# Two-layer encoder trunk on one core: sums of squares of the differential heads and the memory key heads taken from split squares as two float32r products

## The reference, cut to what matters

```python
def rms_norm(x, g):
    xf = x.astype(jnp.float32)
    y = xf * lax.rsqrt(jnp.mean(xf * xf, axis=-1, keepdims=True) + EPS)
    return (y * g.astype(jnp.float32)).astype(x.dtype)

def cross_attention(h, m, w_q, w_kv, w_o, q_norm, k_norm):
    ...
    kv = (m @ w_kv).astype(f32).reshape(bsz, m.shape[1], 2, X_HEADS, X_DH)
    k = rms_norm(kv[:, :, 0], k_norm)

def diff_attention(h, w_in, q_norm, k_norm, lq1, lk1, lq2, lk2, sub_norm, lambda_init):
    ...
    o = jnp.moveaxis(o, 0, 1).reshape(bsz, L, DIFF_HEADS, DIFF_DV)
    o = rms_norm(o, sub_norm) * (1.0 - lambda_init)
```

## Time and profile before

| | |
|---|---|
| runs, median of 3 | 2396.83 us (2396.76 to 2397.51) |
| the profiled execution: span from first to last instruction | 2394.8 us |
| the runs' median above that span | 2.0 us |
| PE busy / PEld busy | 2384.4 us (100%) / 2019.2 us (84%) |
| DVE busy / ACT busy | 1548.8 us (65%) / 1169.1 us (49%) |
| chain that ended last, by engine | PE 87%, DVE 2%, ACT 1% |
| mean DMA throughput | 122 GB/s |
| mean granted PE clock | 1.000 |

### The profile page before, as it was taken

The page is one execution under the profiler, slowest core; times in us unless marked ns, Lnnn a source line. Parts: engine busy times, 40 slices in busy tenths (PEclk is TensorE's granted clock), DMA queues, the critical chain, the costliest instruction groups (busy, mean ns, idle before and its releaser), DMA issues.

```text
span 2394.8 us, 34669 instructions
## 1 busy us (share of the span) xinstructions
PE 2384.4 (100%) x13751; PEld 2019.2 (84%) x13751; DVE 1548.8 (65%) x2626; ACT 1169.1 (49%) x2070; POOL 0.2 (0%) x4
## 2 busy tenths in 40 slices
PE   9999999999999999999999999999999999999999
PEld 6988877888889888998788888888888898888887
DVE  8999668776577876664665448858985565533332
ACT  5334455555435565545453436636764453533432
POOL 0000000000000000000000000000000000000000
PEclk9999999999999999999999999999999999999999
DMA  5446533563224654443225223332234323433232
GB/s 201 106 98 163 211 110 94 171 207 116 69 87 151 193 188 129 134 139 99 79 93 171 88 92 122 93 100 97 90 102 146 122 80 120 126 97 97 97 97 88
DMA packets 109696, 291.30 MB, mean 122 GB/s; under 512 B 18944, under 2 KB 40576, under 8 KB 108256
## 3 DMA queue, kind: packets, MB, share of 16 engines
q1 hardware_dynamic: 100832, 264.83, 35.0%
q10 hardware_dynamic: 8704, 24.25, 3.2%
HBM read 267.45 MB, written 19.50 MB: 120 GB/s over the span
## 4 chain that ended last, share of the span: by engine, by line
PE 87%; DVE 2%; ACT 1%; issue 0%; ACTq 0%
PE ps L1524 67%; PE ps L1510 5%; PE ps L1515 3%; PE ps L1638 2%; PE ps L1595 2%; PE ps L1620 2%; PE ps L1662 1%; PE ps L1651 1%; PE ps L1608 0%; PE ps L1669 0%; PE ps L2034 0%; PE ps L2101 0%; PE ps L1538 0%; DVE wlo L1486 0%; PE ps L1550 0%
## 5 line engine op out<-in xcount | busy, mean ns | idle before, releaser
L1481 ACT ACTIVATE whi<-wraw 128x1024 fp32r<-128x1024 f32 x430 | 452.0, 1052 | 170.3 <-PE ps L1524 126.0
L1524 PE MATMUL ps<-in_hP,whi 128*128 128x512 f32 x1336 | 533.2, 399 | 1.7 <-DVE in_lP L1936 0.9
L1486 DVE TENSOR_TENSOR wlo<-wraw,whi 128x1024 fp32r<-128x1024 f32 x430 | 522.9, 1218 | 0.2
L1524 PE MATMUL ps<-in_hP,wlo 128*128 128x512 f32 x1336 | 520.9, 390 | 0.0
L1524 PE MATMUL ps<-in_lP,whi 128*128 128x512 f32 x1336 | 520.2, 389 | 0.0
L1524 PE MATMUL ps<-hid_P,whi 128*128 128x512 f32 x1024 | 317.1, 391 | 0.0
L1524 PEld LDWEIGHTS ps<-in_hP,whi 128*128 128x128 f32 x1336 | 250.9, 188 | 60.6 <-issue 5.9
L1524 PEld LDWEIGHTS ps<-in_hP,wlo 128*128 128x128 f32 x1336 | 250.8, 188 | 53.4
L1524 PEld LDWEIGHTS ps<-in_lP,whi 128*128 128x128 f32 x1336 | 251.0, 188 | 51.5 <-issue 1.4
L1524 PE MATMUL ps<-in_S,whi 128*128 128x256 f32 x1536 | 285.6, 287 | 0.0
L1869 DVE TENSOR_TENSOR x<-ps,x 128x256 f32<-128x256 f32 (+1 forms) x192 | 107.0, 557 | 262.2 <-PE ps L1524 260.6
(11 more groups left out here) (506 smaller groups left out, 3511.0 us busy)
## 6 DMA issues: line engine op xcount, KB each, us to landing
wraw<-wt SPq DMA_DIRECT2D x432, 512.0 KB, 3.5
wraw<-wt ACTq DMA_DIRECT2D x17, 512.0 KB, 4.2
k_scratch<-region_P SPq DMA_DIRECT2D x16, 256.0 KB, 3.1
v_scratch<-vtmp SPq DMA_DIRECT2D x32, 128.0 KB, 3.7
x<-x_in SPq DMA_DIRECT2D x4, 768.0 KB, 6.8
x<-x_in SPq DMA_DIRECT2D x2, 1536.0 KB, 7.1
mix_mem<-mem_in ACTq DMA_DIRECT2D x1, 2048.0 KB, 15.2
region_S<-k_scratch ACTq DMA_DIRECT2D x2, 1024.0 KB, 6.9
```

The source lines that it names most:

```text
L1481: nc.scalar.activation(whi[:, (n + 3) % NHI, :, :], wraw[:, ws(n), :, :], ACT.Copy).then_inc(wh.sem, 1)
L1486: nc.vector.tensor_tensor(wlo[:, ws(n), :, :], wraw[:, ws(n), :, :], whi[:, (n + 3) % NHI, :, :].bitcast(F32), ALU.subtract).then_inc(wr.s ...
L1524: last = nc.tensor.matmul(ps[:, m % 2, 0:N[prod.g]], w_[:, k, :], x_[:, k, :], start=(k == 0 and j == 0), stop=(k == KT - 1 and j == 2))
```

## The change

Both sums are taken from split squares. The float32 matmul against ones becomes two float32r matmuls against `ones_r`, a float32r copy of the same matrix: one for the high part of the squares and one for the low part, summed in PSUM. The parts are made by two new operations per head:

* ACT copies the square (differential heads) or the added squares (memory key heads) to a float32r tile, the high part.
* DVE subtracts the high part from the square and writes the low part in place.

For a memory key head the high part goes to `sq_l["P"][:, 0]`, the place of `ringP[:, 0]`, whose square has been added by then; that place is therefore now in use until the sum is done, and ACT's next write to it waits for the sum (`ssum`) instead of for the addition (`kad`).

```diff
@@ pe_post, memory key head
-                    pe.wait_ge(z["kad"].sem, prod.kad + h + 1)
-                    nc.tensor.matmul(ps[:, 2, :], ones, ring[g][:, 1, :], start=True, stop=True).then_inc(z["ssum"].sem, 1)
+                    pe.wait_ge(z["sql"].sem, prod.ksl + h + 1)
+                    nc.tensor.matmul(ps[:, 2, :], ones_r[:, :], sq_l[g][:, 0, :], start=True, stop=False)
+                    nc.tensor.matmul(ps[:, 2, :], ones_r[:, :], sq_l[g][:, 1, :], start=False, stop=True).then_inc(z["ssum"].sem, 1)
@@ pe_diff, differential head
-                    pe.wait_ge(z["sqd"].sem, a.sq + h + 1)
-                    nc.tensor.matmul(ps[:, 2, 0:N[g]], ones, ring[g][:, 0, :], start=True, stop=True).then_inc(z["ssum"].sem, 1)
+                    pe.wait_ge(z["sql"].sem, a.sl + h + 1)
+                    nc.tensor.matmul(ps[:, 2, 0:N[g]], ones_r[:, :], sq_h[g][:, :], start=True, stop=False)
+                    nc.tensor.matmul(ps[:, 2, 0:N[g]], ones_r[:, :], sq_l[g][:, 0, :], start=False, stop=True).then_inc(z["ssum"].sem, 1)
@@ act_tile, memory tile two places later
-                        elif j == 0:
-                            a.wait_ge(z["kad"].sem, prod.kad + was // 2 + 1)
@@ new, called on ACT at the start of the slot after the odd tile
+            def act_mem_high(a, t):
+                prod, i, m = t
+                if prod.kind == "mem" and i < KT and i % 2 == 1:
+                    a.wait_ge(gs["P"]["kad"].sem, prod.kad + i // 2 + 1)
+                    nc.scalar.activation(sq_l["P"][:, 0, :], ring["P"][:, 1, :], ACT.Copy).then_inc(gs["P"]["qad"].sem, 1)
@@ act_diff_copy
-                    nc.scalar.activation(ring[g][:, 0, :], ps[:, 6 + h % 2, 0:N[g]], ACT.Square).then_inc(z["sqd"].sem, 1)
+                    act_chain(nc.scalar.activation(ring[g][:, 0, :], ps[:, 6 + h % 2, 0:N[g]], ACT.Square))
+                    nc.scalar.activation(sq_h[g][:, :], ring[g][:, 0, :], ACT.Copy).then_inc(z["sqd"].sem, 1)
@@ new, called on DVE right behind low() in the slot after the odd tile
+            def dve_mem_low(v, t):
+                prod, i, m = t
+                if prod.kind == "mem" and i < KT and i % 2 == 1:
+                    v.wait_ge(gs["P"]["qad"].sem, prod.ksh + i // 2 + 1)
+                    nc.vector.tensor_tensor(sq_l["P"][:, 1, :], ring["P"][:, 1, :], sq_l["P"][:, 0, :].bitcast(F32), ALU.subtract)\
+                        .then_inc(gs["P"]["sql"].sem, 1)
@@ dve_diff_prob, at its start
+                if d_.last(t - 4):
+                    h = (t - 4) // BL[g]
+                    v.wait_ge(z["sqd"].sem, d_.sq + h + 1)
+                    nc.vector.tensor_tensor(sq_l[g][:, 0, :], ring[g][:, 0, :], sq_h[g][:, :].bitcast(F32), ALU.subtract)\
+                        .then_inc(z["sql"].sem, 1)
@@ once, at the start of DVE's program
+                    nc.vector.tensor_copy(ones_r[:, :], ones)
```

More of the change, by code:

```diff
@@ L997, in trunk_tail @@
             ones64_r = sb("ones64_r", [P, P], F32R, on=fl)
+            ones_r = sb("ones_r", [P, P], F32R, on=fl)
             y = {g: sb(f"y{g}", [P, N[g]], on=fl) for g in "PS"}
@@ L1133, in __init__ @@
                     self.ob = ofree.base
-                    self.sq = z["sqd"].take(DH)
+                    self.sq, self.sl = z["sqd"].take(DH), z["sql"].take(DH)
                     self.an, self.ah, self.ar = z["an"].take(DH), z["ah"].take(DH), z["ar"].take(DH)
@@ L1189, in __init__ @@
                     self.sq, self.kad, self.ksc = z["sqd"].take(KT), z["kad"].take(XH), z["ksc"].take(XH)
+                    self.ksh, self.ksl = z["qad"].take(XH), z["sql"].take(XH)
                     self.vtr, self.vcp = z["vtr"].take(KT), z["vcp"].take(KT)
@@ L2408, in _ @@
                             nc.scalar.activation(lam[:, 2:4], ps[:, 7, 0:2], ACT.Exp).then_inc(lam_a.sem, 1)
+                        if before is not None:
+                            act_mem_high(a, before)
                         if q_first(t, steps):
@@ L2496, in _ @@
                             lows = t[2] + NHI - 1
+                        if before is not None:
+                            dve_mem_low(v, before)
                         if before is not None and before[0].kind == "up" and before[0].wide is not None:
```

## The result

The changed kernel takes 2400.91 us (median of 21 runs, 2398.32 to 2401.89), the kernel before, run beside it, 2396.81 us (21 runs, 2396.49 to 2397.51). The ratio is 1.0014, with a 95% interval of 1.0008 to 1.0020: slower by 4.1 us. The forecast was 2396.4 us. The result lies just inside the range that was to leave out 2 cases in 10 (2391.5 to 2401.0), and outside the range that the forecast's own bounds gave (2394.8 to 2400.6). The time has moved, and the forecast said that it would not. The runs fall into two groups, six from 2398.3 to 2398.7 us with a mean granted clock of 0.999 and fifteen from 2400.1 to 2401.9 us with 0.998 (one 0.997).

A forecast was written before the change was run, and what follows sets the result against it. PE was taken as the bound. Memory heads -2.0, P -3.2, S -1.5 and two waits +3.9 and +2.4 gave -0.4 us: span 2394.4, forecast 2396.4 us, own range 2394.8 to 2400.6, 2-in-10-out range 2391.5 to 2401.0.

The forecast's parts named there:

- What bounds the kernel: Whole kernel: PE is busy 2384.4 of 2394.8 us, so time changes only there and new waits cost full length.
- What a sum costs on PE: On PE, the float32r pair saves 0.40 us per memory key or P head and 0.19 per S head.
- Rival D: The pair isn't cheaper between float32 matmuls, for instance by draining the array at each switch; 2401.1 us; chance 0.05.
- Head 4: Layer 0's last memory head: its 0.40 us is lost as PE's later wait grows from 0.72 to 1.1 us.
- The two waits: PE waits for DVE's subtraction at layer 1's first and third memory key heads, about 4.5 and 2.7 us.
- Rival A: The waits at layer 1's first and third memory heads don't happen or cost little; 2389.3 us; chance 0.11.
- The P heads' subtraction: DVE's low part for differential heads of P is ready 0.4 us before PE comes, costing nothing.
- rival C: DVE's subtraction for the P heads is late, costing 0.6 us each, +4.8; 2401.2 us; chance 0.05.
- Price: +3.9 us: Layer 1's first memory key head: subtraction late behind GLA products and a weight split, net +3.9 us.
- Price: +2.4 us: Layer 1's third memory key head: subtraction late behind the chain of states and a weight split, +2.4 us.
- rival B: PE's clock falls in one or both layer 1 waits; 2398.4, 2400.4 or up to 2404.4 us; chance 0.13.
- The price of a spell: Time lost per fall of PE's clock, read from the program's start as half of 4.00 us: +2.0 us.

The follow-up runs named there:

- experiment 4: Changed kernel with the new pair for the 16 differential sums only, memory key sums as before: 2392.12 us, ratio 0.9981 to the kernel before.
- experiment 9: Changed kernel, float32 sum kept for layer 0's last and layer 1's first and third memory key heads: 2390.02 us, ratio 0.9972 to the kernel before.
- experiment 10: Changed kernel, float32 sum kept for layer 1's first and third memory heads, ACT's inverse root before its next-tile copy for layer 0's last: 2389.68 us.
- experiment 1: Changed kernel with 18 and 10 useless matmuls on PE ahead of the waits at layer 1's first and third memory heads: 2396.83 us.
- experiment 6: Changed kernel, but layer 1's third memory key head keeps its float32 sum, leaving only the first one's wait: 2396.20 us.
- experiment 2: Changed kernel with 10 and 5 useless matmuls on PE ahead of the waits at layer 1's first and third memory heads: 2398.02 us.
- experiment 7: Changed kernel, but layer 1's first memory key head keeps its float32 sum, leaving only the third one's wait: 2394.29 us.
- experiment 8: Changed kernel with DVE's subtraction directly behind the addition for layer 1's first and third memory heads, ahead of the GLA steps: 2393.57 us.

## Why the prediction was wrong, step by step

- *What bounds the kernel*: right. All cheaper sums but head 4's showed in the span, and the waits added came out in full.
- *What a sum costs on PE*: right. The pair of head 2 and the next instruction start at 270.78 and 271.23, 0.45 us; a P head gained 0.39 (3.15 / 8), an S head 0.19 (1.55 / 8). Rival D is refuted by experiment 4, which gains 4.5. In the rows of a P head one thing was not as assumed, without effect on the sum:

```profile
1651.11 1.06 PE L1665 MATMUL ps<-at,region_P 128*128 128x128 f32 x8
1651.92 0.48 PE L1672 MATMUL ps<-sq_hP,ones_r 128*128 128x512 f32 x1
1652.23 0.40 PE L1673 MATMUL ps<-sq_lP,ones_r 128*128 128x512 f32 x1
1652.56 0.70 PE L1641 MATMUL ps<-region_P 64*128 64x512 f32 x2
```

The pair's first matmul is followed after 0.31 us, not 0.23, so that the pair and the step to the scores are 0.64 where 0.55 was assumed. But it also starts 0.81 us after the value products, where the float32 one started 0.89 us after them (1644.20 and 1645.09 in the trace before).

- *Head 4*: right in its mechanism, a little small in size: the wait grew by 0.60 us to 1.32, not by 0.40 to 1.1, and the changed kernel's lead shrank from 1.16 to 1.00 us there, so that head 4 costs 0.16 where the sum had it at nothing. Experiments 9 and 10 show the chain as described.
- *The two waits*: right in place, cause and size. Idle 4.76 and 2.71 us against about 4.5 and 2.7 forecast, +3.9 and +2.5 on the path in experiment 1, where the clock stays up. Rival A is refuted.
- *The P heads' subtraction*: right in that no sum waits (rival C is refuted by the list of waits). It ends 0.9 us before PE comes in the first head, 0.4 in the next five, and 0.15 and 0.2 in the last two, where the prediction had the time to spare alike in the first seven.
- *The step that failed* is the price of the waits of heads 5 and 7, "Price: +3.9 us" and "Price: +2.4 us". Each was taken as the shift of the instructions behind it at an unchanged clock. In the profiled execution the lower clock added 2.4 us behind head 5 and 1.5 us behind head 7, and these 3.9 us are the whole difference between the span of 2398.6 and the 2394.4 forecast, but for 0.3 us. Experiment 1 shows that it is the idleness that costs them. The place was named in rival B, whose case of two spells said 2400.4 against 2400.91 measured, but it was given a chance of 0.13 and left out of the forecast's own bounds. That its total came so near is in part luck: it had 2.0 us for each spell.
- *Why its chance was too small*: the argument against it was that a gap of 0.72 us leaves the clock alone. That row says nothing on gaps of 4.6 and 2.8 us. The only rows in which PE worked after a longer idle stretch, showed the lower clock. The Trainium skill, "TensorE: Matmul & The Clock Gate", Part 1, gave the same warning, and the traces agree with it for the gap of 4.8 us (in all the runs of experiment 6, by their times and mean clocks) and go further: gaps of 2.3 to 2.7 us brought the clock down in part of the runs.
- *The price of a spell* was read as 2.0 us from the start of the program; it measured 2.4 and 1.5 us in the profiled execution, and 1.4 to 3.0 us over the runs of the experiments.

One thing stays open: why the same gap brings a fall in one execution and not in the next (experiments 2, 7 and 8). No run was made to tell that.

## What to carry to other kernels

A wait put on a full PE costs its length and, where the clock falls, half of the working time until it is back. Gaps of 2.3 to 4.8 us had that second price here, in part or all of the executions, and gaps of up to 1.5 us did not in the profiled ones; for the longer gaps put it into the sum and not into a rival. Before an operand is made by one more step on another engine, look for the slots in which that engine is late already, and leave those as they are: two exceptions of 24 turned a loss of 4.1 us into a gain of 6.4. Where such a wait can't be avoided, useless matmuls in it can be worth more than they cost (4.1 us in experiment 1).

## What the runs showed of the hardware that had not been expected

Idle gaps on PE of 2.3, 2.4 and 2.7 us brought the granted clock to 0.50 in some executions of a program and not in others (experiments 8, 2 and 7), while a gap of 1.5 us beside them left it at 1.00 in the profiled execution, as did one of 1.32 us ahead of head 4's transposes in the profile after (window 334 to 338 us). In the gap of 4.8 us the clock fell 3.0 us after PE had stopped (0.69 in the window that ends with it). After the gaps of 2.3 and 2.4 us in the profiled executions it fell only when PE had been at work again for 0.8 and 1.2 us (experiments 8 and 2), so that the whole spell lay on work. The clock came back while PE was at work, after 5.1 us of it behind head 5 and after 3.0 us behind head 7. A float32r pair 512 wide takes 0.45 us where a float32 matmul takes 0.86; behind float32 products the second of the pair starts 0.31 instead of 0.23 us after the first, and the first 0.08 us earlier than the float32 matmul did.
